# The scan of a gated delta rule, rewoven: three streams a lane on a grid of 14 steps, PSUM banks shared between lanes, one decay in place of two

## What is computed

```
gc = cumsum(g)                                     # within a chunk
decay = where(incl, exp(gc[c] - gc[s]), 0)
lmat = where(strict, (k*beta) @ k.T * decay, 0)
u, w = triangular_solve(I + lmat, [beta*v, beta*k*exp(gc)])
aqk = q @ k.T * decay
for each chunk:                                    # the chain, in order
    v_new = u - w @ S
    o = (q*exp(gc)) @ S + aqk @ v_new
    S = S*exp(gc[-1]) + (k*exp(gc[-1] - gc)).T @ v_new
```

## Time and profile before

| | us |
|---|---|
| median of three runs | 3905.01 (3898.2 to 3907.04) |
| the profiled execution, own time | 3902.9 |
| its span | 3901.6 |
| scan, first matmul to the start of z | 386.7 to 674.6 |
| z on TensorE | 674.6 to about 709.1 |

### The profile page before, as it was taken

The page is one execution under the profiler, slowest core; times in us unless marked ns, Lnnn a source line. Parts: engine busy times, 40 slices in busy tenths (PEclk is TensorE's granted clock), DMA queues, the critical chain, the costliest instruction groups (busy, mean ns, idle before and its releaser), DMA issues.

```text
span 3901.6 us, 72360 instructions
## 1 busy us (share of the span) xinstructions
PE 3579.2 (92%) x31740; PEld 2309.2 (59%) x31740; DVE 1674.8 (43%) x2942; ACT 1183.8 (30%) x2153; POOL 1407.4 (36%) x1243
## 2 busy tenths in 40 slices
PE   7998777999999998988999999899888888889998
PEld 3755566434445455554555555355677676648887
DVE  1245343145562224444333334543665666433334
ACT  3254222232221553342100000212566665420002
POOL 1320343023231225565433332245344444235444
PEclk9999687999999999999999999899999999999999
DMA  5431000531111114421112111222000000032221
GB/s 193 139 117 33 2 2 12 184 124 46 57 33 65 60 43 162 156 83 44 54 54 65 54 57 62 81 100 90 16 16 16 16 16 4 14 100 89 91 88 66
DMA packets 196435, 263.78 MB, mean 68 GB/s; under 512 B 6135, under 2 KB 151671, under 8 KB 194072
## 3 DMA queue, kind: packets, MB, share of 16 engines
q1 hardware_dynamic: 188960, 241.74, 18.7%
q10 hardware_dynamic: 7160, 17.41, 1.2%
HBM read 246.55 MB, written 12.58 MB: 66 GB/s over the span
## 4 chain that ended last, share of the span: by engine, by line
PE 52%; ACT 6%; DVE 4%; issue 3%; POOL 1%; DMA 0%; ACTq 0%; DVEq 0%; SPq 0%; POOLq 0%
PE ps L238 41%; PE ps L3219 2%; PE ps L771 2%; ACT mem L848 1%; PE ps L382 1%; PE ps L798 1%; PE ps L786 1%; PE ps L489 1%; DVE mem L829 1%; PE ps L3738 1%; POOL mem L3521 0%; ACT mem L858 0%; PE ps L498 0%; PE ps L3746 0%; ACT mem L3154 0%
## 5 line engine op out<-in xcount | busy, mean ns | idle before, releaser
L238 PE MATMUL ps<-mem 64*64 64x64 f32 (+4 forms) x25184 | 2673.8, 300 | 145.0 <-POOL mem L3122 28.7
L238 PEld LDWEIGHTS ps<-mem 64*64 64x64 f32 (+1 forms) x25184 | 1733.1, 154 | 1093.6 <-issue 573.5
L3122 POOL TENSOR_TENSOR mem<-mem 128x256 f32<-128x256 f32 (+1 forms) x264 | 225.6, 868 | 353.5 <-PE ps L238 174.4
L866 POOL TENSOR_SCALAR mem<-mem 128x768 f32<-128x768 f32 (+2 forms) x128 | 219.3, 1727 | 199.0 <-DVE mem L832 198.9
L2363 ACT ACTIVATE mem<-ps 128x384 f32<-128x384 f32 (+1 forms) x80 | 35.7, 446 | 779.2 <-PE ps L238 736.7
L2350 POOL TENSOR_TENSOR mem<-mem 128x512 f32<-128x512 f32 (+1 forms) x80 | 100.5, 1257 | 445.3 <-PE ps L238 368.8
L596 POOL TENSOR_TENSOR mem<-mem 128x512 f32<-128x512 f32 (+1 forms) x72 | 75.3, 1066 | 430.0 <-ACT mem L591 426.8
L2374 DVE TENSOR_TENSOR mem<-mem,ps 128x384 f32<-128x384 f32 (+1 forms) x80 | 39.9, 499 | 415.2 <-PE ps L238 415.2
L3219 PE MATMUL ps<-mem 128*128 128x128 f32 x960 | 177.9, 303 | 31.4 <-DVE mem L3144 20.3
L3152 ACT ACTIVATE mem<-ps 128x256 f32<-128x256 f32 (+1 forms) x220 | 101.7, 462 | 199.8 <-PE ps L3219 199.5
L3144 DVE TENSOR_TENSOR mem<-mem,ps 128x256 f32<-128x256 f32 (+1 forms) x220 | 109.5, 514 | 120.9 <-PE ps L238 120.2
(11 more groups left out here) (337 smaller groups left out, 4079.7 us busy)
## 6 DMA issues: line engine op xcount, KB each, us to landing
mem<-i_mod_w SPq DMA_DIRECT2D x48, 1024.0 KB, 6.8
mem<-i_ffn_wg SPq DMA_DIRECT2D x22, 1024.0 KB, 5.3
mem<-i_ffn_wu SPq DMA_DIRECT2D x22, 1024.0 KB, 5.4
mem<-i_e_w_in SPq DMA_DIRECT2D x16, 1024.0 KB, 6.3
mem<-i_o_w_in SPq DMA_DIRECT2D x16, 1024.0 KB, 5.4
mem<-i_ffn_wd SPq DMA_DIRECT2D x16, 1024.0 KB, 5.0
mem<-i_e_mod_w SPq DMA_DIRECT2D x12, 1024.0 KB, 11.8
mem<-i_o_mod_w SPq DMA_DIRECT2D x12, 1024.0 KB, 6.8
```

Of the source, the lines that this page charges most:

```text
L238: ins = e.h.matmul(out, l, r, start=(i == 0), stop=(i == n - 1))
L866: K.pool.h.tensor_scalar(w, w, stat(i, o, 1), None, MUL).then_inc(*nm.up(tag, i, o))
L3122: K.pool.h.tensor_tensor(m3(self.slot(l)), self.lraw, bm(C(K, f"cm{self.d}", l, 64), 2 * self.np), MUL).then_inc(*self.mk.up(key, l))
```

## The change

- A lane is now three streams that run side by side: the front of the next tile, the inverse, and the chain. `at(d, i) = 12 + 7 d + 14 i` gives the step of the first level of unit (d, i); its first product is 2 steps earlier, its front begins 12 steps earlier, its chain 5 steps later. So a tile takes 14 steps of a lane, and lane 1 is 7 behind.
- In the front `kk` comes 2 steps after `gate`, and `kq` 6 steps after `kk`. In the chain `k` is at step 5, `u` at 13, `o` at 14, `s` at 15 after `at`.
- Banks: each lane has two of its own for the inverse (0 and 1, 2 and 3). Bank 4 takes the turns and first products of both lanes, bank 5 `gate` and `kk` of both, bank 6 `k`, `kq` and `o`, bank 7 `u` and `s`.
- X is no longer clamped twice: ScalarE takes |X| and exp(-|X|) into one buffer E, which serves both products. Where the masks keep entries X has one sign, so this is the same decay. GpSimd's two clamps of a tile are gone.
- `Lc` and `Lo` are doubled. The sixth level multiplies `Lo`, now scaled with beta by GpSimd, with U itself and no longer with `ub`.
- `z` begins at step 94 and is spread, two of its k-steps to a step.

```diff
--- before.py
+++ after.py
+    more = [K.alloc(512) for _ in range(2)]
     RI = [{"U": w[0], "T": w[1], "P": w[2], "Lm": w[3:5]} for w in own]
-    Lc, Lo, OD = [w[5] for w in own], [w[6] for w in own], ot[:, 4:8, :]
-    gm, em, Rb, vn, v2, sd = ([K.alloc(512) for _ in range(2)] for _ in range(6))
-    Xb = [[K.alloc(512) for _ in range(2)] for _ in range(2)]
+    Lc, Lo, OD = [(own[d][5], more[d][:, 0:256]) for d in range(2)], [(own[d][6], more[d][:, 256:512]) for d in range(2)], ot[:, 4:8, :]
...
+    TB, FB, KB, UB = 4, 5, 6, 7
...
+        return Inverse64(K, ("dn", d, i), ("dn", d, i - 1) if i else None, RI[d], d, d, m3(Lc[d][i % 2]), 2, K.id64, TB, TB)
...
+    def front_pe(d, i):
         tt, x, c0 = place(d, i)
-        a, b, c = 3 * d, 3 * d + 1, 3 * d + 2
+        vacant(K, FB)
+        K.pe.wait_ge(*gate.at(d, i))
+        K.pe.h.matmul(K.ps[FB], C(K, "ones"), gm[d], start=True, stop=True).then_inc(*pr.up(d, i, "gate"))
+        K.busy[FB] = [(ux, (d, i, "x"))] + ([(ex, (d, i, "qs"))] if x else [])
+        yield from idle(2)
+        vacant(K, FB)
+        for h in range(4):
+            ins = K.pe.h.matmul(K.ps[FB][:, HS[h]], kT[:, h, c0:c0 + 128], kT[:, h, c0:c0 + 128], start=True, stop=True)
+        ins.then_inc(*pr.up(d, i, "kk"))
+        K.busy[FB] = [(ux, (d, i, "L"))]
+        yield from idle(6)
+        if x:
+            vacant(K, KB)
+            for h in range(4):
+                ins = K.pe.h.matmul(K.ps[KB][:, HS[h]], kT[:, h, c0:c0 + 128], qT[:, h, c0:c0 + 128], start=True, stop=True)
+            ins.then_inc(*pr.up(d, i, "kq"))
+            K.busy[KB] = [(ux, (d, i, "rt"))]
...
+    def front_dve(d, i):
+        tt, x, c0 = place(d, i)
+        E, s, q = Eb[d][i % 2], 1 - d, d
+        K.dve.wait_ge(*pr.at(d, i, "gate"))
+        K.dve.h.tensor_tensor(h3(E), h3(K.ps[FB]), bc(GC[:, d, tt], 128), SUB).then_inc(*ux.up(d, i, "x"))
+        yield
+        if x:
+            K.dve.wait_ge(*ex.at(d, i, "qs"))
+            K.dve.h.tensor_tensor(h3(qs[d][i % 2]), h3(qs[d][i % 2]), qT[:, :, c0:c0 + 128], MUL).then_inc(*ux.up(d, i, "qs"))
+        yield from idle(2)
+        K.dve.wait_ge(*pr.at(d, i, "kk"))
+        K.dve.wait_ge(*ex.at(d, i, "E"))
+        if i >= 2:
+            last = inverse(d, i - 2)
+            K.dve.wait_ge(*last.mk.at(last.key, 5))
+            K.dve.wait_ge(*last.pr.at(last.key, "p", 6))
+        K.dve.wait_ge(*zero.at("Lo", d, i % 2))
+        for e in range(2):
+            K.dve.h.tensor_tensor(m3(Lc[d][i % 2])[on(e)], part(K.ps[FB], e, e), part(E, e, e), MUL).then_inc(*ux.up(d, i, "L", e))
+        K.dve.h.tensor_tensor(m3(Lo[d][i % 2])[on(s)], part(K.ps[FB], s, q), part(E, s, q), MUL).then_inc(*ux.up(d, i, "L"))
+        yield from idle(5)
+        if x:
+            K.dve.wait_ge(*pr.at(d, i, "kq"))
+            if i >= 2 and place(d, i - 2)[1]:
+                K.dve.wait_ge(*ch.at(d, i - 2, "o"))
+            K.dve.h.tensor_tensor(rt[d][i % 2], K.ps[KB], E, MUL).then_inc(*ux.up(d, i, "rt"))
+
+    def front_act(d, i):
+        tt, x, c0 = place(d, i)
+        E = Eb[d][i % 2]
+        K.act.wait_ge(*ux.at(d, i, "x"))
+        if x:
+            if i >= 2 and place(d, i - 2)[1]:
+                K.act.wait_ge(*ch.at(d, i - 2, "o"))
+            K.act.h.activation(qs[d][i % 2], K.ps[FB], ACT.Exp).then_inc(*ex.up(d, i, "qs"))
+        yield
+        K.act.h.activation(E, E, ACT.Abs).then_inc(*ex.up(d, i, "abs"))
+        K.act.wait_ge(*ex.at(d, i, "abs"))
+        K.act.h.activation(E, E, ACT.Exp, scale=-1.0).then_inc(*ex.up(d, i, "E"))
...
+    def front_pool(d, i):
+        tt, x, c0 = place(d, i)
+        inv = inverse(d, i)
+        yield from idle(4)
+        K.pool.wait_ge(*ux.at(d, i, "L"))
+        K.pool.h.tensor_tensor(m3(Lc[d][i % 2]), m3(Lc[d][i % 2]), strength(d, tt, slice(0, 128), 128), MUL).then_inc(*scl.up(d, i, "L"))
+        yield
+        K.pool.h.tensor_tensor(m3(Lo[d][i % 2]), m3(Lo[d][i % 2]), strength(d, tt, slice(0, 128), 128), MUL).then_inc(*scl.up(d, i, "Lo"))
+        yield
+        K.pool.wait_ge(*scl.at(d, i, "L"))
+        inv.masked(0)
+        yield
+        inv.masked(1)
+        if i < 5:
+            gates(d, i + 1)
+        yield from idle(2)
+        if x:
+            K.pool.wait_ge(*ux.at(d, i, "rt"))
+            K.pool.h.tensor_tensor(h3(rt[d][i % 2]), h3(rt[d][i % 2]), tri(d), MUL).then_inc(*scl.up(d, i, "rt"))
+
...
+    def inverse_pe(d, i):
+        inv, a = inverse(d, i), 2 * d
+        s, q, U, T, P = 1 - d, d, RI[d]["U"], RI[d]["T"], RI[d]["P"]
+        yield from inv.first(TB)
+        yield
+        yield from inv.levels(a, TB)
+        vacant(K, TB)
+        K.pe.wait_ge(*inv.u.at(inv.key, 5))
+        turn(K, K.ps[TB], U, 0, 2).then_inc(*inv.pr.up(inv.key, "v", 6))
+        K.busy[TB] = [(inv.cp, (inv.key, "T", 6))]
...
+        K.pe.wait_ge(*scl.at(d, i, "Lo"))
         for g in range(2):
             for h in range(2):
                 w = slice((2 * g + h) * 64, (2 * g + h) * 64 + 64)
-                ins = K.pe.h.matmul(K.ps[a][on(h), on(g)], Lo[d][on(s), w], part(ub[d][i % 2], s, s)[:, 2 * g + h, :], start=True, stop=True)
...
-        K.pool.h.tensor_scalar(em[d], X, 0.0, None, MAX).then_inc(*scl.up(d, i, "em"))
-        if x:
-            K.pool.wait_ge(*scl.at(d, i, "em"))
-            K.pool.h.tensor_scalar(X, X, 0.0, None, MIN).then_inc(*scl.up(d, i, "xm"))
...
+            product(KB, (lambda h: kT[:, h, c0:c0 + 128], lambda h: S[d][:, HS[h]])).then_inc(*ch.up(d, i, "k"))
+            K.busy[KB] = [(cs, (d, i, "r"))]
+        yield from idle(8)
+        vacant(K, UB)
+        if i:
             K.pe.wait_ge(*cs.at(d, i, "R"))
...
-    def lane(unit, chain, d):
-
-        for _ in range(8 * d):
-            yield
-        for i in range(7):
-            yield from weave(*([unit(d, i)] if i < 6 else []), *([chain(d, i - 1)] if i else []))
...
+    def at(d, i):
+
+        return 12 + 7 * d + 14 * i
...
+            K.pool.h.memset(Lo[d][j], 0.0).then_inc(*zero.up("Lo", d, j))
...
+            for k in range(KT):
+                ins = K.pe.h.matmul(K.ps[m % 2], w[:, k, m % 2 * 128:m % 2 * 128 + 128], hap(k, 0, NX), start=k == 0, stop=k == KT - 1)
+                if k == KT - 1:
+                    ins.then_inc(*zl.up("ez0", m))
+                if k % 2:
+                    yield
...
+    def lanes(inv, front, chain, z):
+
+        units = [(d, i) for i in range(6) for d in range(2)]
+        run(*(later(at(d, i) - 2, inv(d, i)) for d, i in units), *(later(at(d, i) - 12, front(d, i)) for d, i in units),
+            *(later(at(d, i) + 5, chain(d, i)) for d, i in units), later(at(0, 5) + 12, z()))
...
+    lanes(inverse_pe, front_pe, chain_pe, z_pe)
...
+    def first(self, b):
+
+        K, key = self.K, self.key
+        vacant(K, b)
+        K.pe.wait_ge(*self.mk.at(key, 0))
+        many(K, self.np, BY_E, chunky(K.ps[b]), (chunky(self.slot(0)), lambda i, e, h: self.id64[64 * e:64 * e + 64, :])).then_inc(*self.pr.up(key, "t"))
+        K.busy[b] = [(self.u, (key, 0))]
+        yield
...
```

More of the change, by code:

```diff
@@ new lines, in inverse_act, with inverse_pool @@
+        yield from inv.act(2 * d)
+        K.act.wait_ge(*inv.pr.at(inv.key, "v", 6))
+        K.act.h.activation(RI[d]["T"], K.ps[TB][:, 0:256], ACT.Copy).then_inc(*inv.cp.up(inv.key, "T", 6))
+        K.act.wait_ge(*inv.pr.at(inv.key, "p", 6))
+        K.act.h.activation(RI[d]["P"][:, 0:128], K.ps[2 * d][:, 0:128], ACT.Copy, scale=-1.0).then_inc(*inv.cp.up(inv.key, "P", 6))
+    def inverse_pool(d, i):
+        inv = inverse(d, i)
+        yield from idle(2)
+        for l in range(2, 6):
+            inv.masked(l)
+            yield from idle(2)
@@ L1627, in chain_pool, with idle, later @@
             K.pool.h.tensor_tensor(h3(sd[d]), h3(S[d]), bc(EGL[:, d, tt], 128), MUL).then_inc(*csd.up(d, i))
-    def lane(unit, chain, d):
-        for _ in range(8 * d):
+        yield
+    def idle(n):
+        for _ in range(n):
             yield
-        for i in range(7):
-            yield from weave(*([unit(d, i)] if i < 6 else []), *([chain(d, i - 1)] if i else []))
-    zero = K.sig("un_zero", "pool")
+    def later(n, g):
+        yield from idle(n)
+        yield from g
+    def at(d, i):
+        return 12 + 7 * d + 14 * i
     for d in range(2):
@@ L1648, in z_pe @@
                 n, w = K.take(kn(256))
[L1649 to L1651 removed]
+            vacant(K, m % 2)
+            for k in range(KT):
[3 more added lines that the diff above has]
+                if k % 2:
+                    yield
+            K.busy[m % 2] = [(zs, ("ez0", m))]
             if m % 2:
                 K.spent(n, zl, "ez0", m)
[L1654 removed]
     def z_act():
@@ L3076, with __init__ @@
 class Inverse64:
-    def __init__(self, K, key, before, R, lane, d, lraw, np_, id64):
+    def __init__(self, K, key, before, R, lane, d, lraw, np_, id64, first=None, turned=None):
         self.K, self.key, self.before, self.R, self.lane, self.d = K, key, before, R, lane, d
```

(1 more changed line is left out.)

264 lines of the change are left out of this document (75 added, 189 removed).

## The result

| | before | after |
|---|---|---|
| median | 3903.61 us (3898.2 to 3907.04) | 3804.39 us (3800.84 to 3805.09) |
| ratio, 95% interval | | 0.9747 (0.9734 to 0.976) |
| span of the profiled execution, mean clock | 3901.6 us, 0.957 | 3803.2 us, 0.972 |

A forecast was written before the change was run, and what follows sets the result against it. TensorE bounds the scan, losing 65 us idle and often running at the low clock. Start, half-periods, z and 5 us for unplaced waits give a 99 us gain from 3902.9: 3804, as median 3806; range 3786 to 3868.

The forecast's parts named there:

- Waits: TensorE's waits in the scan for masks (28.7 us), R (9.0) and vn (4.7) go, 42.4 us together.
- The wait of 0.4 a half-period: In the step after gate, ScalarE's copy of the next level's product comes late at 2.4 GHz; 0.4 us a half-period.
- Half-periods: Seven steps of the scan with nothing waiting take 14.1 us at 2.4 GHz, 25.1 at 1.2; about 24 before.
- Clock: TensorE's clock in the scan is at 2.4 GHz from the fourth unit on.
- the fifth rival: The high clock comes in the scan's second unit already: 14 us less than the sum, 3792; chance 0.11.
- The sum: Start, half-periods, z and 5 us for unplaced waits: gain 99 us, 3804, as median 3806; chance 0.50.
- The 5 us set aside for unplaced waits: Allowance added to the sum because the dense RWKV scan is 88% busy and not 97%; 5 us.
- Start: Lane 0's first product waits behind lane 1's gate and kk and begins at about 399.0, before at 396.1.
- End: z with the rest of lane 1 in its gaps takes 38.0 us and ends at 604.7.
- some 20: Expected sign: GpSimd's work in the scan falls by some 20 us.
- the clock row's fifth digit: Expected sign in the changed profile: fifth and sixth digit of the page's clock row at 9.
- a sign of being wrong: The prediction would be wrong if the clock is at 0.50 in long busy stretches.

The follow-up runs named there:

- the decay alone: Kernel before with only |X| and exp(-|X|) on ScalarE in place of GpSimd's two clamps and two exponentials; ratio to before 1.0001.
- the paired kernel: Kernel after with k one step earlier, right behind kk, and s one step later, so large groups stand in pairs; ratio to before 0.9791.
- the two fillers: Kernel before with unread products ahead of each unit's first product, large ones in one run (ratio 0.9965), small ones in another (1.0063).
- the small filler: Kernel before with 46 unread 64x64 products ahead of each unit's first product; ratio to before 1.0063.
- the filler ahead of the scan: Kernel after with unread large products in TensorE's gaps from 377 to 400 us; ratio to before 0.9738, region 6.2 us shorter than after.
- the large filler: Kernel before with two unread 128x512 matmuls ahead of each unit's first product; ratio to before 0.9965, region 300.4 us against 331.1.
- the two edits that moved k: Kernel after with k one step earlier and s one later (ratio to before 0.9791), and with k alone one step earlier (0.9762).
- the kernel with late fronts: Kernel after with each front four steps later (8 instead of 12 ahead of the unit); 3834.14 us, ratio to before 0.9836.

## Why the prediction was right

The forecast was 3806 and the median is 3804.39. The mechanism held: the waits go, and the clock is high. That the number came within 2 us is luck, since steps of it were wrong by 7 us and in opposite directions. Step by step:

- *Waits.* The masks', R's and vn's go, as I had it. But I had read wrongly why the masks were late. GpSimd's clamp and the exponential behind it were not the cause, and the decay alone took only 2.0 us off the waits. In the kernel before, too, the exponential that `Lc` needs ended at 563.8 and VectorE came to `Lc` at 570.7, behind o. The wait of 0.4 a half-period for ScalarE's copy, the next one that I named, does not come in full half-periods; only 2.3 us of it stand in the whole scan.
- *Half-periods.* I had 14.1 + 0.4 for a full one; from the gate at 473.64 to that at 533.89 there are four, 15.06 each and without a wait. The 0.4 was the wrong term, and another was too small: I priced kk and kq at 0.89 by the earlier trace rows, where a large group stands behind them. Standing alone they take 1.09. In the paired kernel kk with k behind it took 1.00. So each border between large and small costs about 0.1 us, two for a group alone. Half-periods without o are 13.4 to 13.9 (gates at 432.34, 446.27, 459.71, 473.64), where I took 12.8.
- *Clock.* 2.4 GHz came at 413.7 us, in the first half-period behind gate and kk, and not in the fourth unit. That is about where the second unit begins, so it is the fifth rival's clock; it priced this at 14 us less, 3792.
- *The sum* came out all the same, since these errors have opposite signs. From the first product to z's first matmul (567.20) the trace has 167.2 us, the sum 167.7. The first six half-periods, which I had at 85.7 with the low clock in three of them, took 78.6 (12.7, 11.6, 13.0, 13.9, 13.4 and 13.9, by VectorE's subtraction of the first product). The four full ones took 60.2 for 58.0, and the last stretch 28.3 for 24.0, with two waits of 0.5 us for ScalarE's copy where fronts and chains run out. So 7.1 us too many stand against 6.5 too few, and the early clock brought half of the rival's 14. The 5 us set aside for unplaced waits were not needed in the scan. They happen to cover most of the 1.5 us by which it began later in this execution and of the 6.1 in the rest, below, for which I had set nothing aside.
- *Start.* The first product is at 400.05, against 399.0; the whole scan had shifted by 1.5 us ahead of it (gate at 388.26 and not 386.71), so this was right to 0.5.
- *End.* z's last matmul ends at 604.4, against 604.7; z's part takes 37.2 and not 38.0.
- *GpSimd* has 100.3 us in the scan and had 115.0: 14.7 less and not some 20. The scaling of Lo takes 0.763 each where I took 0.62, and two of its other groups (level masks, mask on rt) have become longer too. It sets nothing.
- *Signs.* Of what I had named, the clock row's fifth digit is 8 and not 9. The clock was at 0.51 for 13.7 us of 85% busy work, a sign of being wrong that showed only at the start.
- *What follows z* I had as moved only. The region is 106.0 us shorter and the span 98.4. The rest behind the norm's start is 3187.2 before and 3193.3 after, but 3190.7 in the second execution of the kernel after, and from 3185.8 to 3203.2 over all kernels. So nothing systematic is shown to be given back.
- *The reason for the clock.* That the gaps of about 2 us made it fall is shown by the two fillers. In the kernel before, the clock's records in the trace have it fall during, or within 2 us behind, nine of the eleven mask waits that found it high; behind the one at 572.2 it stayed up. That large groups bring it back sooner than small ones, which I had read from the earlier trace rows, fits the small filler's first 56 us at 0.50, but is not isolated by a run.

The Trainium skill (TensorE: Matmul & The Clock Gate, Part 1) says that sustained activity releases the clock and idleness brings it back to 1.2 GHz. For the second half this case agrees (0.71 to 0.94 by filling the gaps); for the first it does so only with a qualification, since with the small filler TensorE was 80% busy for 56 us at 0.50.

What stays open: how much of the clock's early rise comes from gate and kk being large, and how much from the absence of waits around them; whether the 6 us of the filler ahead of the scan reach the whole time; and how much of the large filler's 30.7 us in the region is its own, since the time has 13.7.

## What to carry to other kernels

When streams share an in-order engine, count for each handover what stands between the producer's instruction and the reader's: here the two edits that moved k left one handover a unit uncovered, and paid 0.52 and 1.33 us for it twelve times. A gap of about 2 us on TensorE can cost more than its length, since the clock may fall behind it (in the kernel with late fronts it fell behind gaps of 1.0 us too); unread products in the gap are a quick test, if they fit. The worth of an edit depends on the order around it (the decay: nothing before, 14 us after), so test it on the order that it will live in.
